# Requesting ScalarE's quarter of x before the identity and the norm weights, on one queue

## The reference: what is computed

```python
def rms_norm(x, g):
    x32 = x.astype(jnp.float32)
    y = x32 * lax.rsqrt(jnp.mean(x32 * x32, axis=-1, keepdims=True) + RMS_EPS)
    return (y * g.astype(jnp.float32)).astype(x.dtype)
...
    for l in range(DEPTH):
        x = x + 0.5 * swiglu(rms_norm(x, ffn1_norm[l]), ffn1_w_up[l], ffn1_w_down[l])
        x = x + hybrid_mixer(rms_norm(x, mix_norm[l]), w_in[l], na_rel_bias[l], w_branch_a[l],
                             w_branch_b[l], w_out[l], pos)
        x = x + 0.5 * swiglu(rms_norm(x, ffn2_norm[l]), ffn2_w_up[l], ffn2_w_down[l])
    return rms_norm(x, final_norm)
```

## Time and profile before

| | us |
|---|---|
| median of 3 runs | 1146.61 |
| lowest and highest | 1146.02 and 1146.76 |
| the profiled execution, its own time | 1146.13 |
| its span in the profile | 1144.3 |
| PE busy in the span | 1134.3 (99%) |
| DVE busy | 764.7 (67%) |
| ACT busy | 584.3 (51%) |

### The profile page before, as it was taken

How to read it: one execution, slowest core, us unless ns; L and a number is a source line. 1 busy time by engine, 2 the same in 40 slices (tenths; PEclk the granted TensorE clock), 3 DMA queues, 4 the chain that set the end, 5 groups by cost and what they waited for, 6 DMA issues and landing times.

```text
span 1144.3 us, 17172 instructions
## 1 busy us (share of the span) xinstructions
PE 1134.3 (99%) x6707; PEld 955.5 (84%) x6707; DVE 764.7 (67%) x981; ACT 584.3 (51%) x781; POOL 76.2 (7%) x116
## 2 busy tenths in 40 slices
PE   9999999999999999999999999999999999999997
PEld 6888888888888888888888888888888888888886
DVE  6866666756666776666686666677565677666665
ACT  6544445555553654444464444465555546544442
POOL 3622100000120000000000000000001200000000
PEclk9999999999999999999999999999999999999999
DMA  9866654744643565555546555556446545555551
GB/s 295 275 219 229 201 183 151 253 154 142 195 178 133 179 218 192 186 195 197 178 164 210 184 183 188 202 188 197 151 144 201 202 144 199 201 191 183 187 180 37
DMA packets 148246, 214.34 MB, mean 187 GB/s; under 512 B 9344, under 2 KB 114016, under 8 KB 147936
## 3 DMA queue, kind: packets, MB, share of 16 engines
q1 hardware_dynamic: 142960, 205.28, 52.9%
q0 software_dynamic: 4560, 6.97, 2.1%
q10 hardware_dynamic: 672, 1.37, 0.4%
HBM read 210.75 MB, written 5.12 MB: 189 GB/s over the span
## 4 chain that ended last, share of the span: by engine, by line
PE 98%; DVE 1%; issue 1%; ACT 0%; POOLq 0%; POOL 0%; DVEq 0%; ACTq 0%
PE banks L1273 25%; PE banks L1207 16%; PE banks L1209 16%; PE banks L1208 16%; PE banks L1271 14%; PE banks L1270 4%; PE banks L1421 1%; PE banks L1245 1%; PE banks L1384 1%; PE banks L1407 1%; PE banks L1453 1%; PE banks L1396 0%; PE banks L1442 0%; PE banks L1238 0%; PE banks L1475 0%
## 5 line engine op out<-in xcount | busy, mean ns | idle before, releaser
L864 DVE TENSOR_TENSOR w_lo<-raw,w_hi 128x2048 fp32r<-128x2048 f32 x190 | 437.3, 2303 | 190.6 <-ACT w_hi L629 190.5
L629 ACT ACTIVATE w_hi<-raw 128x2048 fp32r<-128x2048 f32 x190 | 363.8, 1916 | 209.5 <-PE banks L1209 207.3
L1273 PE MATMUL banks<-a_both,w_hi 128*128 128x512 f32 x1232 | 439.6, 396 | 0.0
L1271 PE MATMUL banks<-a_both,w_lo 128*128 128x256 f32 x1408 | 364.3, 279 | 0.0
L1271 PEld LDWEIGHTS banks<-a_both,w_lo 128*128 128x128 f32 x1408 | 265.4, 189 | 14.9
L1273 PEld LDWEIGHTS banks<-a_both,w_hi 128*128 128x128 f32 x1232 | 231.2, 188 | 47.4
L1207 PE MATMUL banks<-w_hi,a_both 128*128 128x512 f32 (+1 forms) x448 | 176.6, 394 | 0.0
L1209 PE MATMUL banks<-w_hi,a_both 128*128 128x512 f32 (+1 forms) x448 | 171.6, 383 | 0.0
L1208 PE MATMUL banks<-w_lo,a_both 128*128 128x512 f32 (+1 forms) x448 | 171.2, 382 | 0.0
L1207 PE MATMUL banks<-w_hi,hT_hi 128*128 128x512 f32 x320 | 125.0, 390 | 0.0
L1209 PE MATMUL banks<-w_hi,hT_lo 128*128 128x512 f32 x320 | 124.5, 389 | 0.0
(11 more groups left out here) (119 smaller groups left out, 927.9 us busy)
## 6 DMA issues: line engine op xcount, KB each, us to landing
raw<-ffn_w_up_dram SPq DMA_DIRECT2D x172, 512.0 KB, 4.1
raw<-w_in_dram SPq DMA_DIRECT2D x92, 512.0 KB, 4.4
raw<-ffn_w_down_dram SPq DMA_DIRECT2D x88, 512.0 KB, 4.0
raw<-w_out_dram SPq DMA_DIRECT2D x16, 512.0 KB, 4.1
raw<-w_branch_b_dram SPq DMA_DIRECT2D x8, 512.0 KB, 4.5
raw<-ffn_w_up_dram SPq DMA_DIRECT2D x8, 256.0 KB, 4.6
bias_rows<-bias_kinds POOLq DMA_DIRECT2D x32, 64.0 KB, 4.0
bias<-bias_rows SPq DMA_DIRECT2D x2, 1024.0 KB, 7.7
```

Of the source, the lines that this page charges most:

```text
L629: act.activation(w_hi[slot][:, :], raw[slot][:, :], ACT.Copy).then_inc(hi_done, 1)
L864: dve.tensor_tensor(w_lo[slot][:, :], raw[slot][:, :], w_hi[slot][:, :].bitcast(F32), ALU.subtract).then_inc(lo_done, 1)
L1271: mm = pe.matmul(pair[:, b, 0:SEQ], w_lo[slot][:, at:at + P], a_hi[:, k, :], start=False, stop=False)
L1273: mm = pe.matmul(pair[:, b, :], w, both, start=False, stop=k == KT - 1)
```

## The change

ACT's program begins with three requests, four transfers in all. The two transfers of x's quarter 1 now come first, and the identity and the norm weights after them. Nothing else changes: the other engines' programs are the same, and so are the sizes, the semaphores and the waits.

```diff
         @block.scalar
         def _(act):
+            load_x(act, 1)
             act.dma_start(ident, consts[:, C_IDENT:C_ALL]).then_inc(ident_loaded, 16)
             act.dma_start(gain_rows[0:DEPTH * PHASES * KT, :],
                           gains[0:LAST, :].rearrange("g (k p) -> (g k) p", p=P)).then_inc(gain_rows_loaded, 16)
-            load_x(act, 1)
```

## The result

| | before | after |
|---|---|---|
| median of 7 runs each, us | 1146.76 | 1150.16 |
| lowest and highest | 1146.02 and 1147.61 | 1149.08 and 1150.77 |
| ratio of the times, 95% interval | | 1.003, 1.0021 to 1.0040 |
| profiled execution, its own time | 1146.13 | 1150.77 |
| its span | 1144.3 | 1149.0 |

The change costs 0.3%, outside the predicted range of 1146.2 to 1148.8. The direction of the forecast was right; its size, 0.8 us, was not. The profiled execution is the slowest of the seven, so its numbers lie at the upper end; that of the kernel before lies 0.63 us under its median.

A forecast was written before the change was run, and what follows sets the result against it. PE bounds the kernel, busy 1134.3 of 1144.3 us, so only start-up matters. Terms 0 + 0.8 + 0 + 0 = +0.8 us on the median of 1146.61 gave about 1147.4, range 1146.2 to 1148.8.

The forecast's parts named there:

- The one-for-one rule: Whole kernel: PE waits for nothing of size after start-up, so a shift of the first product shifts the end equally.
- The earlier quarter: Start-up: quarter 1 requested 0.90 us earlier can remove only PE's 0.42 us idle, covered by ACT's work: 0.
- the identity and the norm weights later: Start of ACT's queue: norm weights requested 1.25 us later, landing after 3.1 us, delay PE's transposes: +0.8 us.
- The bound of 4.3 us: Upper end for the norm weights' landing, from ACT's transfer beside SP's weights: landing at 6.74, cost +1.95 us.
- The +0.25: Start of ACT's queue: cost if only issue time counts, 1.25 us displaced less 1.01 of slack.
- The small return from the clock: PE's quarter 0 transposes, starting later, might partly run at 2.4 GHz: at best 0.3 us back, not counted.
- a clock that stays low: Rival: PE's 0.8 us pause before the transposes keeps TensorE at 1.2 GHz, 1149.8; chance 0.06, loss above 2.3 us 0.04.
- No cost: Rival: the norm weights land by 4.8, within PE's zeros, so the time stays 1146.6; chance 0.12.
- the earlier quarter pays: Rival: norm weights on time and quarter 1 had been held by PE; wins at most 0.42 us, 1146.2; chance 0.04.
- four runs in a hundred: Forecast chance of 0.04 that the changed kernel is slower by over 0.2%, above 1148.9 us.
- a slack read from one execution (0.18 us here): Start-up: quarter 1's transposes end at 7.20, 0.18 us before ACT comes to them, so its late landing costs nothing.

The follow-up runs named there:

- the second profile of before: The kernel before, unchanged, run once more with a profile: 1147.52 us, span 1145.7.
- the second profile: The changed kernel, unchanged, run once more with a profile: 1149.25 us (one run).
- norm weights, x, identity: The kernel before with only the identity moved behind quarter 1, the norm weights staying first: 1148.07 us, ratio 1.0012.
- before, table load first: The kernel before with ACT's table load and first small activation moved ahead of its requests: 1149.58 us, ratio 1.0022.
- changed, SP waits: The changed kernel, with SP waiting for the norm weights to land before requesting the first weights and all behind them: 1150.25 us (one run).
- half ahead: The changed kernel with only quarter 1's first half ahead of the identity and norm weights, the second half behind them: 1147.91 us, ratio 1.0007.
- identity, x, norm weights: The kernel before with only the norm weights moved behind quarter 1, the identity staying first: 1147.39 us, ratio 1.0008.
- late requests, nothing ahead: The kernel before, with ACT waiting for its table load and a small activation before requesting anything, quarter 1 last: 1149.65 us (one run).
- changed, quarter 2 first: The changed kernel, with SP requesting quarter 2 of x ahead of the first two parts of the first weights: 1148.00 us, ratio 1.0008.
- changed, four executions: The changed kernel twice (1150.16, 1149.25 us), with 22 zeros (1148.98), and with PE turning the norm weights after quarters 0 and 1 (1149.06).
- 22 zeros: The changed kernel with 22 multiplications of zeros at the start of PE's program instead of 8: 1148.98 us, ratio 1.0016.

## Why the prediction was right or wrong

**The one-for-one rule held.** The span less the start of the first product is 1133.9 us in the first profile of before, 1133.8 in the changed kernel's, and 1133.7 to 1134.2 in sixteen of the eighteen profiles (1134.6 and 1134.7 in the other two).

**The earlier quarter was worth nothing, as costed.** Its landing moved from about 6.5 to about 6.1 (1.4 + 4.7), and PE did not even ask for it before 8.75. But the reading of the earlier trace rows was too firm: in the second profile of before ACT does wait for quarter 1.

**The step that failed is the price of "the identity and the norm weights later".** The prediction took a landing of 3.1 us with 4.3 as the upper end, from a request at 2.44. It was 5.7 from a request at 2.92 (4.8 in the second profile), so PE's transpose of the norm weights started 4.0 us later in the first profile and 3.1 in the second, not 0.8. Two things were wrong. First, the requests themselves: the pair of x occupied ACT's queue for 1.40 us instead of 1.22, the identity for 0.69 instead of 0.39 (1.24 and 0.86 in the second profile, with the same sum). Second, and larger, the nearest rows were chosen by kind of transfer, not by what was requested before them on both queues. Counted in that way (own bytes included, all sizes as in the rows, one execution each where no number of them stands):

| kernel | KB requested until then | norm weights land at |
|---|---|---|
| norm weights, x, identity | 152 | 2.6 |
| before, four executions | 216 | 3.8 to 4.2 |
| before, table load first | 344 | 4.5 |
| changed, SP waits | 600 | 5.7 |
| half ahead | 728 | 5.6 |
| identity, x, norm weights | 856 | 6.4 |
| late requests, nothing ahead | 856 | 6.3 |
| changed, quarter 2 first | 856 | 7.1 |
| changed, four executions | 1112 | 7.7 to 8.6 |

The row for this was in the prediction: ACT's second half of quarter 1 landed at 6.5 with the same 856 KB requested until then. From 3.8 at 216 KB to 6.5 at 856 KB is 0.42 us for 100 KB; at 1112 KB that gives 7.6 us (an estimate), and a wait of 2.8. The bound of 4.3 us was the duration of a transfer with 256 KB less in this count, and no upper end at all.

By the Trainium skill, "DMA: Bandwidth & Descriptors", section "SWDGE vs HWDGE vs iDMA", all issuing engines share the same DMA engines. The trace agrees: without SP's weights in flight ACT's norm weights took 2.7 us instead of 5.7. The +0.25 that the prediction drew from this section counts only the time of issuing, and measured was a landing 4.8 us later (3.8 to 8.6): a small transfer behind a backlog isn't priced by its own issue.

**The small return from the clock had the wrong sign.** I left it at 0, with the rival of a clock that stays low at 0.06. That rival's mechanism came, though not as it was described: in the first profile the clock did not stay low, it had risen and fell at 8 us in the pause, and PE then ran at 1.2 GHz to nearly 15 us. In the second it was low until about 12.5. It cost about 1.3 us in the first profile (6.43 against the 5.11 with 22 zeros) and 0.6 in the second (5.75). The rival had 3.2 us against 10.38, of which 0.8 was the landing, so 2.4 for the clock. Its time of 1149.8 is close to the measured 1150.16 by luck: the larger part of the loss is the landing, which it priced at 0.8.

A part of the clock's cost is made by the zeros between the groups of transposes. In the first profile DVE began the low part of the first weights at 13.56, so by the earlier trace rows the product could have started near 14.3 (an estimate). It started at 15.18, behind the second five zeros, which took 1.78 us. No run leaves these zeros out.

**Rivals and chances.** "No cost" and "the earlier quarter pays" fell. That four runs in a hundred would be over 1148.9 was far too few, since both unknown prices lay on the same side and one can bring the other: a longer wait is also a longer pause.

**Still open.** Why ACT's requests occupy its queue longer in this order was not tried. The table of bytes gives an order, not a law: at 856 KB it spreads over 0.8 us, and the second half of quarter 1, with the same 856 KB, landed between 6.5 and 7.6 in four executions, of which the prediction had the earliest. Bytes were not separated from the number of packets. How much of the low clock is due to the pause is open too: with 22 zeros and no pause it was high, but the second profile of the kernel before had it low after a pause of 0.75 us.

## What to carry to other kernels

At a start where several queues request at once, list all requests of all queues in order of time with their bytes, and expect a small transfer to land after most of what was requested before it; put what the first waiting engine needs first, however small the slack of the large one looks. A moved request must be priced by the traffic of the new place, not by its own old duration. And a slack read from one execution (0.18 us here) is not a cover: a second profile of the same kernel showed it gone. A landing varies as well: the same requests brought the norm weights at 7.7 us in one execution and at 8.6 in another.

## What the runs showed of the hardware

The same transfer of 24 KB took between 1.8 us (first request of all, in the order norm weights, x, identity) and 5.7 us. The same kernel took 1146.02 to 1147.61 us, and part of that is when quarter 1 lands (6.54 or 6.97) and when TensorE's clock rises: zeros at 7 to 10 us took 0.25 each in one profile of before and 0.47 in the other. In the changed kernel the granted clock was 1.00 from 5 to 8 us, with PE idle, and 0.50 from 8 to 14. Fourteen more zeros at the head, which in their profile ended 0.6 us after the norm weights had landed (7.9), brought the changed kernel from +3.4 to +1.9 us.
